# Gated expert rows added onto the output in DRAM, and one-hot products for the fixed experts of the last two tiles

## The reference, cut to what matters

```python
def hierarchical_moe(u, ...):
    g_p, g_idx = lax.top_k(softmax(xt @ w_rg + b_rg), 1)      # one group of 4
    e_p, e_idx = lax.top_k(softmax(e_logits[g_idx]), 2)       # two of its 8 experts
    gates = g_p * e_p / jnp.sum(e_p, axis=-1, keepdims=True)
    ...                                                       # tokens sorted by expert
    hdn = jax.nn.silu(xb @ w_gate[e]) * (xb @ w_up[e])        # 1024 -> 512
    ys = hdn @ w_down[e]                                      # 512 -> 1024
    out = jax.ops.segment_sum(ys * gate, token)

h = h + attention_and_conv(...)                               # called h1 below
h = h + hierarchical_moe(rms_norm(h), ...)                    # rms_norm(h1): u2 below
return h[:, N_META:]
```

## Time and profile before

| | |
|---|---|
| median of 3 runs | 1305.84 us (1304.88 to 1308.56) |
| profiled execution, its own time | 1306.04 us |
| its span | 1304.2 us |
| busy: TensorE, VectorE, ScalarE, POOL | 1153.1, 640.7, 545.4, 214.9 us |
| granted TensorE clock, mean | 0.961 |
| DMA traffic | 291.56 MB, of it 42.65 MB in POOL's queue |
| chain that ended last: PE, DMA, DVE, ACT | 58%, 21%, 9%, 6% of the span |

### The profile page before, as it was taken

The page is one execution under the profiler, slowest core; times in us unless marked ns, Lnnn a source line. Parts: engine busy times, 40 slices in busy tenths (PEclk is TensorE's granted clock), DMA queues, the critical chain, the costliest instruction groups (busy, mean ns, idle before and its releaser), DMA issues.

```text
span 1304.2 us, 18197 instructions
## 1 busy us (share of the span) xinstructions
PE 1153.1 (88%) x6700; PEld 867.8 (67%) x6700; DVE 640.7 (49%) x930; ACT 545.4 (42%) x820; POOL 214.9 (16%) x257
## 2 busy tenths in 40 slices
PE   4899999998998888989887999999999889898960
PEld 4899988898995566666665787655555555555530
DVE  6322233334335556666655886544444445455516
ACT  6212132143335455444432775455444544555520
POOL 4000001131100011111013212222212222221210
PEclk9999999999998799999997999999999999999995
DMA  9410004423004222222085799999999999999969
GB/s 255 98 66 1 1 33 147 175 100 131 1 2 129 78 82 83 81 77 74 17 318 191 284 372 368 420 424 397 404 387 410 394 388 392 400 398 388 365 243 369
DMA packets 66251, 291.56 MB, mean 224 GB/s; under 512 B 10696, under 2 KB 36328, under 8 KB 53648
## 3 DMA queue, kind: packets, MB, share of 16 engines
q1 hardware_dynamic: 48320, 243.91, 49.3%
q0 software_dynamic: 16720, 42.65, 8.7%
q10 hardware_dynamic: 1152, 4.19, 0.8%
HBM read 270.62 MB, written 37.92 MB: 237 GB/s over the span
## 4 chain that ended last, share of the span: by engine, by line
PE 58%; DMA 21%; DVE 9%; issue 6%; ACT 6%; SPq 1%; POOL 0%; DVEq 0%; ACTq 0%; POOLq 0%
DMA wu<-in_w_up 16%; PE ps L1007 9%; PE ps L1008 9%; PE ps L1009 9%; PE ps L1350 4%; PE ps L1302 3%; PE ps L1304 3%; PE ps L1303 3%; PE ps L1088 3%; PE ps L1102 2%; PE ps L1120 2%; DMA y<-expert_rows 2%; DMA wd<-in_w_down 2%; PE ps L1291 2%; DVE probs L2005 1%
## 5 line engine op out<-in xcount | busy, mean ns | idle before, releaser
L2057 DVE TENSOR_TENSOR wu_low<-wu,wu_high 128x2048 fp32r<-128x2048 f32 x36 | 81.1, 2288 | 56.8 <-ACT wu_high L1635 56.8
L1316 PE MATMUL ps<-wg,xa 128*64 128x512 f32 x224 | 102.1, 598 | 0.0
L1316 PE MATMUL ps<-wu,xa 128*64 128x512 f32 x224 | 102.1, 598 | 0.0
L1635 ACT ACTIVATE wd_high<-wd 128x2048 fp32r<-128x2048 f32 x36 | 66.8, 1905 | 81.3 <-DMA wd<-in_w_down 79.4
L2057 DVE TENSOR_TENSOR wd_low<-wd,wd_high 128x2048 fp32r<-128x2048 f32 x36 | 81.2, 2288 | 36.2 <-ACT wd_high L1635 35.9
L1635 ACT ACTIVATE wu_high<-wu 128x2048 fp32r<-128x2048 f32 x36 | 66.9, 1907 | 69.8 <-DMA wu<-in_w_up 69.8
L1007 PE MATMUL ps<-uh,w_high 128*128 128x342 f32 (+1 forms) x256 | 88.1, 344 | 4.4 <-DVE w_low L1760 4.4
L2057 DVE TENSOR_TENSOR wg_low<-wg,wg_high 128x2048 fp32r<-128x2048 f32 x36 | 81.0, 2289 | 19.1 <-ACT wg_high L1635 19.1
L1009 PE MATMUL ps<-uh,w_low 128*128 128x342 f32 (+1 forms) x256 | 87.7, 343 | 0.0
L1008 PE MATMUL ps<-ul,w_high 128*128 128x342 f32 (+1 forms) x256 | 87.7, 343 | 0.0
L1635 ACT ACTIVATE wg_high<-wg 128x2048 fp32r<-128x2048 f32 x36 | 66.9, 1907 | 25.1 <-DMA wg<-in_w_gate 24.1
(11 more groups left out here) (383 smaller groups left out, 3011.3 us busy)
## 6 DMA issues: line engine op xcount, KB each, us to landing
wg<-in_w_gate SPq DMA_DIRECT2D x32, 2048.0 KB, 17.2
wu<-in_w_up SPq DMA_DIRECT2D x32, 2048.0 KB, 19.5
wd<-in_w_down SPq DMA_DIRECT2D x32, 2048.0 KB, 20.4
u_rows<-u POOLq DMA_DIRECT2D x16, 512.0 KB, 6.0
y<-expert_rows SPq DMA_DIRECT2D x16, 512.0 KB, 12.0
raw_c<-in_w_in SPq DMA_DIRECT2D x5, 1024.0 KB, 6.1
xin<-in_x SPq DMA_DIRECT2D x8, 512.0 KB, 8.2
zx<-in_x POOLq DMA_DIRECT2D x4, 1024.0 KB, 6.7
```

The costliest lines, as they stand in the source:

```text
L1316: last = mm(ps[HALF * n:HALF * (n + 1), 7, :], xa[:, k, :], raw[m][:, 1, k, :], start=(k == 0), stop=(k == KT - 1))
L1635: A(flat_half(wh[m][:, :, :], n), flat_half(raw_kf(m, s), n), ACT.Copy).then_inc(w_high[m], 1)
L2057: return V.tensor_tensor(flat_half(wl[m][:, s, :, :], n), flat_half(raw_kf(m, s), n), flat_half(wh[m][:, :, :], n).bitcast(F32), ALU.subtr ...
```

## The change

1. slot_table holds two numbers a slot, the token's number and its gate's bits (aux gets a last axis of 2); the gate is computed (GT) before a tile is placed, and slot_ready comes from GT instead of S.
2. h1b is stored straight to out. scatter writes to out with `compute_op=ALU.add`, and u2 has one copy in DRAM; a token's two experts now add to the same row. So free_result, the wait for the scatter before, stands ahead of each scatter instead of behind it.
3. take_y multiplies by the gate: the activation's scale is a column of tab, and a register load from gate_col (`value_load`) says which. ScalarE waits before its loop for the table and the columns.
4. The tail is gone: dram_h1, expert_rows, h1t, y0, y1, their loads, the 16 additions and the 8 stores.
5. earlier_rows becomes first_rows: tiles 0 to 5 from the table, loaded when their slots are out; tiles 6 and 7 each by a product FIRST (rank_hot and first_code), the first of them in the tail of extras. The tail's order changes with it, and PLACE stands between the two halves of the first gate product; bexp and the columns are written before wu's second low part.

```diff
-DVE_TAIL = [("O", R7), ("LT", R6), ("N", R7), ("A", R7), ("AL", R7), ("RT", R6), ("GL", 0), ("W0", R7), ("G", R6),
-            ("S", R6), ("GL", 1), ("W1", R7), ("GT", R6), ("U2", R7), ("U0", R7), ("U1", R7), ("L", R7), ("LT", R7),
-            ("RT", R7)]
+DVE_TAIL = [("O", R7), ("LT", R6), ("N", R7), ("A", R7), ("AL", R7), ("RT", R6), ("GL", 0), ("GL", 1), ("W0", R7),
+            ("G", R6), ("W1", R7), ("HOT", R6), ("U2", R7), ("FIRST", R6), ("S", R6), ("GT", R6), ("U0", R7), ("U1", R7),
+            ("L", R7), ("LT", R7), ("RT", R7)]
...
-            for t in range(NT):
-                sp.dma_start(h1t[:, t, :], dram_h1[P * t:P * (t + 1), :]).then_inc(y_in[t], 16)
-            sp.wait_ge(all_out, 1)
...
-                pool.dma_start(dram_h1[P * i:P * (i + 1), :], h1b[:, :]).then_inc(h1_out, 16)
+                pool.dma_start(out[P * i:P * (i + 1), :], h1b[:, :]).then_inc(h1_out, 16)
...
-            pool.dma_start(earlier_rows[:, :], dealt_rows[:, :, 0:FIXED],
-                           allow_slow_non_contiguous=True).then_inc(earlier_in, 16)
...
+                elif i:
+                    pool.wait_ge(slots_out, 16 * 2 * (NT - 2))
+                    pool.dma_start(first_rows[:, :, :].rearrange("p k n -> p (k n)"), dealt_rows[:, :, 0:2 * FIXED],
+                                   allow_slow_non_contiguous=True).then_inc(first_rows_in, 16)
+                    pool.wait_ge(pv_done, UNITS)
...
                 nc.gpsimd.indirect_dma_start(
-                    out=ys[:, :], in_=yb[:, s, :], in_offset=None,
+                    out=out[:, :], in_=yb[:, s, :], in_offset=None,
                     out_offset=bass.IndirectOffsetOnAxis(ap=idxs[:, s:s + 1].bitcast(U32), axis=0),
-                    bounds_check=last_row, oob_is_err=False).then_inc(ys_out[s], 16)
+                    bounds_check=last_token, oob_is_err=False, compute_op=ALU.add).then_inc(ys_out[s], 16)
...
             with pool.Fori(2, last, 2) as i:
                 for s in range(2):
                     gather(i + s + 4, s, 2 * (i + s) + 5)
+                    free_result(1 - s, i // 2 + s)
                     scatter(i + s, s, 2 * (i + s) + 6)
-                    free_result(1 - s, i // 2 + s)
             for s in range(2):
-                scatter(last + s, s, 2 * last + 5 + s)
                 if s == 0:
                     free_result(1, last // 2)
+                else:
+                    pool.wait_ge(ys_out[0], 16 * (last // 2 + 1))
+                scatter(last + s, s, 2 * last + 5 + s)
...
-            def take_y(n_done, n_free, s):
+            def gate(b, half):
+
+                c = act.value_load(gate_col[0:1, bass.ds(b + 1, 1)], min_val=0, max_val=2 * (TABW + TABC))
+                own = slice(0, P) if half is None else slice(HALF * half, HALF * (half + 1))
+                return tab[own, 1:][:, bass.ds(c, 1)].bitcast(F32)
+
+            def take_y(b, n_done, n_free, s):
                 act.wait_ge(done_with["d"][s], n_done + counted["d"][s])
                 act.wait_ge(yb_free, n_free)
-                A(yb[:, s, :], big[:, 5 * 512:7 * 512], ACT.Copy).then_inc(y_taken, 1)
+                A(yb[:, s, :], big[:, 5 * 512:7 * 512], ACT.Copy, scale=gate(b, None)).then_inc(y_taken, 1)
```

More of the change, by code:

```diff
@@ L1731, in _ @@
             silu_half(last + 1)
-            take_y(last // 2 + 1, last + 2, 0)
+            take_y(last, last // 2 + 1, last + 2, 0)
             take_hidden(last + 1)
             take_y_half(last + 1)
-            for t in range(NT):
-                act.wait_ge(fin_ready, t + 1)
-                act.dma_start(out[P * t:P * (t + 1), :], h1t[:, t, :]).then_inc(fin_out, 16)
-            act.wait_ge(fin_out, 16 * NT)
         @block.vector
@@ L1979, in extra @@
                     then(V.tensor_reduce(rank[:, :], rk2[:, :, :], AX.X, ALU.add))
+                elif kind == "CODE":
+                    for k in range(2):
+                        then(V.tensor_scalar(first_code[:, k, :], iota128[:, 0:FIXED], expid[:, k, i:i + 1],
+                                             row_codes[:, i:i + 1], ALU.is_equal, ALU.mult))
+                elif kind == "HOT":
+                    if i == R6:
+                        dve.wait_ge(codes_ready, 2)
+                        extra("CODE", i)
+                    then(V.tensor_scalar(rank_hot[:, 0, :], dealt[:, :], rank[:, 0:1], None, ALU.is_equal))
+                    V.tensor_scalar(rank_hot[:, 1, :], dealt[:, :], rank[:, 1:2], None,
+                                    ALU.is_equal).then_inc(routing_operands, 1)
+                elif kind == "FIRST":
+                    job = ("FIRST", i)
+                    if i == R6:
+                        dve.wait_ge(first_rows_in, 16)
+                        then(V.tensor_copy(first_sum[:, :], first_rows[:, :, 0]))
+                    wait_x_made(dve, job)
+                    if i == R6:
+                        V.tensor_tensor(first_sum[:, :], ps[:, x_bank(job), 0:FIXED], first_sum[:, :],
+                                        ALU.add).then_inc(x_used, 1)
+                    else:
+                        V.tensor_tensor(idxg[:, :], ps[:, x_bank(job), 0:FIXED], first_sum[:, :],
+                                        ALU.add).then_inc(idx_ready, 2)
+                        dve.wait_ge(idx_ready, 2)
+                        dve.sem_inc(x_used, 1)
+                    wait_x_used(dve, job)
                 elif kind == "S":
@@ L2074, in _ @@
             dve.wait_ge(codes_ready, 6)
-            for k in range(2):
-                then(V.tensor_scalar(first_code[:, k, :], iota128[:, 0:FIXED], expid[:, k, R7:R7 + 1],
-                                     last_codes[:, k:k + 1], ALU.is_equal, ALU.mult))
+            wait_x_made(dve, ("FIRST", R6))
+            extra("CODE", R7)
+            then(V.tensor_scalar(free_expert[:, :], expert[:, :], float(FIXED), None, ALU.is_ge))
             extra("G", R7)
-            then(V.tensor_scalar(rank_hot[:, 0, :], dealt[:, :], rank[:, 0:1], None, ALU.is_equal))
-            V.tensor_scalar(rank_hot[:, 1, :], dealt[:, :], rank[:, 1:2], None, ALU.is_equal).then_inc(routing_operands, 1)
-            dve.wait_ge(earlier_in, 16)
-            then(V.tensor_copy(earlier_code[:, :], earlier_rows[:, :]))
+            extra("HOT", R7)
             job = ("CNT", 0)
@@ L2215, in _ @@
             hidden_half(last + 1)
-            for t in range(NT):
-                dve.wait_ge(y_in[t], 48)
-                then(V.scalar_tensor_tensor(h1t[:, t, :], y0[:, t, :], gates[:, 0, t:t + 1], h1t[:, t, :],
-                                            ALU.mult, ALU.add))
-                V.scalar_tensor_tensor(h1t[:, t, :], y1[:, t, :], gates[:, 1, t:t + 1], h1t[:, t, :],
-                                       ALU.mult, ALU.add).then_inc(fin_ready, 1)
 _ORDER = ["x", "meta_tokens", "norm_mix_g", "w_in", "b_forget", "q_norm_g", "k_norm_g", "conv_w", "attn_out_g",
```

187 lines of the change are left out of this document (88 added, 99 removed).

## The result

The changed kernel takes 1315.16 us (median of 14 runs, 1310.75 to 1321.48); the kernel before, beside it, 1305.07 (14 runs). The ratio is 1.0079, with a 95% interval of 1.0062 to 1.0096: slower by 10 us, where 14 us faster was forecast. The profiled execution took 1316.12 us.

The account below looks back on a forecast made before the run. DMA was taken to bind most of the expert stage, TensorE 7% behind, with TensorE idle in the tail. 1306.04 − 30.9 − 5 + 17.2 + 4.5 = 1291.8, so 1291.5 us; range 1270 to 1316.

Parts of the forecast that it names:

- step 3: Expert loop: scatters' additions read 8.4 MB from out at the stage's rate, costing 17 us; bounds 0 and 34.
- Its bound above: Upper bound for the additions in DRAM: two more passes of their bytes, 34 us.
- The sign by which the prediction would have called itself wrong altogether: Expert loop: an accumulating scatter's landing under load being twice that of a plain one.
- the 21 us that the prediction worked out by it: Expert stage: by the skill's rule the scatters' own time doubles, giving 21 us over the stage.
- Step 1: Program end: dropping the tail makes the last scatter's landing the end, gain 30.9 us; bounds 35.6 and 26.
- Step 2: Start of the experts: earlier table rows, first gather and first dynamic load gain 5 us; bounds 0 to 7.
- Step 4: Gates on ScalarE: register loads of 0.74 us per pair cost 4.5 us, half of 9.6; lower bound 0.
- Step 5: Serial scatters on POOL: each waits for the previous landing, cost 0, since the chain just fits within a pair.
- the step's 3.6 us: Scatter chain of one pair: twice about 1.8 us from a landing to the next issue.
- x: Scatter landings in the expert loop: the time an addition lengthens each landing, taken as 1.5 us.
- rival C: Expert loop: the serial scatter chain becomes the bound, some 1300 to 1312 us; binds from x = 2.2; chance 0.3.

Follow-up runs that it names:

- a_plain: The changed kernel with the addition taken out, so scatters overwrite the output's rows: 1274.54 us, ratio 0.9771.
- b_acc: The kernel before with only the addition put in: scatters add onto expert_rows, filled ahead of the loop by 16 stores; 1341.93 us, ratio 1.0306.
- a_half: The changed kernel adding only in the scatters with s = 0, every other block; the others overwrite: 1298.01 us, ratio 0.9930.
- a_narrow: The changed kernel with each adding scatter split in two of half the width, rows of 2 KB: 1319.28 us, ratio 1.0106.
- a_bulk: a_plain with 8.4 MB more of plain reads on SyncE's queue, one load of 128 rows a pair: 1293.34 us, ratio 0.9912.
- a_nogate: The changed kernel without gates and their register loads in ScalarE's copies, the scale being constant 1.0: 1316.15 us, ratio 1.0071.
- a_addlin: a_wrlin with the 14 extra stores of the loop adding onto their rows instead of overwriting: 1310.05 us, ratio 1.0034.
- a_addind: a_wrind with the 14 extra stores of the loop adding onto their rows instead of overwriting: 1310.48 us, ratio 1.0044.
- a_wrlin: a_plain with 15 extra overwriting 512 KB stores from POOL's queue, without indices, onto 128 rows lying together: 1293.61 us, ratio 0.9908.
- b_notail: The kernel before without its tail, the residual stored straight into the output: 1279.89 us, ratio 0.9806.
- a_tail: The changed kernel with the kernel before's tail and overwriting scatters; start, gates and serial scatters stay: 1308.26 us, ratio 1.0025.
- b_serial: The kernel before with one wait moved, so each scatter waits for the one before to land: 1310.58 us, ratio 1.0046.
- a_tail_free: a_tail with the scatters no longer in series: 1310.86 us, ratio 1.0045.
- a_read: a_plain with the same rows gathered once more behind each scatter on POOL's queue, 8.4 MB in all: 1315.72 us, ratio 1.0068.
- a_end: The changed kernel with the last waits for landings on SyncE instead of POOL: 1311.43 us, ratio 1.0042.
- a_wrind: a_wrlin with its 15 extra stores made by indices onto 128 rows 32 KB apart, overwriting: 1292.91 us, ratio 0.9910.
- ap_narrow: a_narrow without the addition, its half-width scatters overwriting: 1278.54 us, ratio 0.9804.

## Why the prediction was wrong

The step that failed is 3, "the additions in DRAM, cost 17 us". Measured were 40.2 ± 3.5 us (a_plain) and 40 ± 4 (b_acc). Its bound above, "two more passes of its bytes, 34", was closer than the value taken. With 40 in its place the sum gives 1314.6, against 1315.2 measured. The mechanism was right as far as it went, only the size was off: the read is paid for, in the stretch where DMA binds, by the byte (a_half, a_narrow), and plain bytes cost what the step said (18.4 us, a_bulk).

What was wrong in its reasoning is that the bytes' price is the whole price. An added row costs its queue 0.20 us more, 25.6 us on each engine on the average, a fifth above the 21.2 us of its bytes; and the program lost 15 us beyond that. Two things move with it, and the runs speak against both as the cause. The weights' queue took 10 us longer per engine, but in b_acc, which loses 40 us too, only 4. The product behind ha cost TensorE 14 us more, at a lower clock (57.6 to 71.8), but in a_nogate, as slow as the changed kernel, it takes 62.4, and in a_half 59.1, 1.5 over a_plain, where 21 us are lost.

A third thing fits the sizes, and no run tests it: how the added rows lie over the 16 DMA engines. The last scatter of the changed kernel moves 58 rows. Of its 16 landings eight come after 2.6 to 2.7 us and eight after 5.3 to 5.9. In a_plain the same scatter's landings come after 2.0 to 2.1 and 3.0 to 3.1 us, and its 58 packets of 4 KB, 0.16 us each, start in waves of eight, 0.16 us apart. So eight engines seem to carry all the rows. The kernel's 32 scatters have 64 valid rows of 128 on the average (27 to 85 each), while every extra store of a_addlin and a_addind has 128. An estimate: 2048 added rows on the same eight engines are 256 on each, and at 0.20 us a row 51 us, of which 40 were lost; 14 stores of 128 rows on all sixteen are 112 on each, 22.5 us, of which 16.5 and 17.5 were lost. Both times about three quarters. The trace does not name a packet's engine, so that the eight are always the same is not shown; a kernel that puts the valid rows of a scatter into other slots would show it. Until then, what makes the kernel's own additions cost two passes stays open. Excluded are indices, spread rows, the gates and the series; a price by the piece is unlikely (a_narrow). The sign by which the prediction would have called itself wrong altogether, landings under load of twice a plain one's, did not come (medians of 13.5 and 11.8 us), so landings do not show this price.

The rule of the Trainium skill that the prediction weighed, in "Collectives: The Full Stack" (the bandwidth ceiling), halves the rate of a reducing DMA by its two source reads. The queue's times roughly agree: a plain stored row costs 0.16 us (a_wrlin against a_plain, 126.3 − 107.2 us for 120 rows an engine), an adding one about 0.36; in the last scatter, with hardly anything beside it, 0.16 and 0.33. But the 21 us that the prediction worked out by it fell short of the 40 us that the program lost.

*Step 1, the tail, −30.9.* The serial last scatter and its longer landing came as said (the last two landings took 6.1 and 5.9 us, 6.5 and 4.6 were taken). POOL's DRAIN, which stood in the trace of before and was overlooked because other work covered it, took 8 of the 35.6 us back. b_notail puts the tail at 25 ± 5; a_plain against a_tail, which have gates, series and start in common but for one copy of u2, at 33 ± 4. Between them lies the forecast, so whether its net size was off the runs can't tell; the drain it had left out is an error all the same.

*Step 2, the start, −5.* The marks came as forecast (gather by 699: 699.64; first dynamic load near 716: 716.92), but idxg only at 698.7, not 696, since the second rank_hot itself moved from 694.23 to 697.11, and the loop kept 2.2 us of the gain. The 4 to 5 us were read off the first loads, and should have been read off the first thing that the pairs wait for.

*Step 4, the gates, +4.5:* −1 ± 4 (a_nogate). The lower of its bounds, 0.

*Step 5, the series, 0:* x came out as taken, at 1.2 to 1.7 us where the step has 1.5 (median landings of 13.5 us against 12.3 before and 11.8 in a_plain). The point from which rival C decides, 2.2, was not reached: two landings and the step's 3.6 us are 30.6, under the pair's 36.4. Pairs did not lengthen in either trace of b_serial. Its times, 5 us over before, speak for a small cost; a_tail against a_tail_free speaks against it. Open within 0 to 5 us.

So the sum of all but step 3 was right: −31.4 forecast, −30 ± 3 measured (a_plain against before). In part this is luck: the start was taken some 3 us too good and the gates some 5 us too dear, and the two nearly cancel. Rival C had the right sign, for a reason that was not there, and 1315.2 lies above its 1300 to 1312, just inside the outer bound of 1316. The wrong sign came from one term, step 3.

## What to carry to other kernels

Where DMA already binds, an addition by the scatter is no free replacement of a read, add and store at the end. Count at least one more pass of its bytes, leave room for two, and look at how the valid rows of a scatter lie over the engines, since that is the candidate left: here 8.4 MB added in the loop cost 40 us, and the tail of 12.6 MB read and 4.2 MB stored, with TensorE idle, cost 25 to 33. The bytes of the tail were moved while nothing else ran, the read of an addition where the DMA share stood at 0.97.

Before a tail is costed as removed, look at what ends beside it: each queue's last entries in the trace of before become the end once their cover is gone. And a control that puts bytes back must put them where nothing of the kernel waits behind them, or it measures the wait (a_read against a_bulk).

## What the runs showed of the hardware

- POOL's DRAIN at the program's end takes 5.6 (a_narrow) to 10.7 us (a_end) in these kernels, 7.7 in the changed one and 9.2 before, and begins when POOL has nothing left; with the final wait moved off POOL, part of it overlaps with the last transfer and 5 ± 3 us come back (a_end).
- The read of an adding DMA is in neither the queue's bytes (38.93 MB against 38.92) nor the page's amount read from DRAM (258.36 MB in both); the queue's time (10.1% against 8.4%) and a lower rate at nearly the same share (372 against 398 GB/s) show it.
- With hardly anything beside it, a plain row of 4 KB takes its DMA engine 0.16 us and an adding one 0.33 (the last scatters of a_plain and of the changed kernel). A scatter of 58 valid rows of 128 keeps about eight engines busy, not sixteen (the same).
- An adding scatter is issued more slowly: 1.6 us of POOL for one at 1292.31, where an overwriting one takes 1.0.
- 8.4 MB in 2048 pieces of 4 KB, plain, cost 18 us read by SyncE's queue (a_bulk); 7.9 MB in 1920 pieces, stored by POOL's, 18 us with indices (a_wrind) or without (a_wrlin). Doubling the number of pieces that overwrite hardly matters (ap_narrow, 4 ± 5 us).
